# One more large matmul per attention slot and per recurrence chunk, into a PSUM tile that the next product overwrites

## What is computed

```python
# recurrence, over chunks of tokens
scores = einsum('bhtk,bhsk,bhtsk->bhts', q, k, decay)
o = einsum('bhts,bhsv->bhtv', scores, v) + einsum('bhtk,bhkv->bhtv', q * exp(G), S)
S = exp(G_last) * S + einsum('bhsk,bhsv->bhkv', k * exp(G_last - G), v)
# stick-breaking attention of the prompt, causal
z = q @ k.T * scale + bias
sp = where(mask, softplus(z), 0);  after = reverse_cumsum(sp) - sp
o = where(mask, exp(log_sigmoid(z) - after), 0) @ v
```

## Time and profile before

| | us |
|---|---|
| median of three timed runs | 4821.75 (4820.92 to 4822.06) |
| the profiled execution's own time | 4756.05 |
| its span from first to last instruction | 4753.9 |
[...]

### The profile page before, as it was taken

How to read it: one execution, slowest core, us unless ns; L and a number is a source line. 1 busy time by engine, 2 the same in 40 slices (tenths; PEclk the granted TensorE clock), 3 DMA queues, 4 the chain that set the end, 5 groups by cost and what they waited for, 6 DMA issues and landing times.

```text
span 4753.9 us, 42732 instructions
## 1 busy us (share of the span) xinstructions
PE 3042.5 (64%) x12504; PEld 1643.8 (35%) x12504; DVE 2842.7 (60%) x6773; ACT 923.8 (19%) x2045; POOL 2378.1 (50%) x2198
## 2 busy tenths in 40 slices
PE   6877786976675777765646667777465545434434
PEld 3545555644441443332213324443122223101111
DVE  6577831212456556656756766566677657766664
ACT  1432111112231113432101113333110001000000
POOL 1011100000346546657766775567767657777675
PEclk8988996656657777776777786567677767767766
DMA  6476952222669878778999998788999889999998
GB/s 244 168 309 263 395 201 83 52 94 71 236 229 366 307 281 318 286 250 331 333 358 356 371 379 299 276 301 322 348 334 387 333 314 362 348 367 375 351 370 318
DMA packets 432901, 1389.01 MB, mean 292 GB/s; under 512 B 67174, under 2 KB 135014, under 8 KB 420382
## 3 DMA queue, kind: packets, MB, share of 16 engines
q0 software_dynamic: 306432, 1216.48, 68.1%
q1 hardware_dynamic: 102094, 144.95, 9.1%
q10 hardware_dynamic: 24144, 24.86, 1.5%
HBM read 1333.57 MB, written 56.86 MB: 292 GB/s over the span
## 4 chain that ended last, share of the span: by engine, by line
POOL 21%; PE 19%; issue 17%; another core or an unknown queue 6%; DVE 5%; DMA 5%; ACT 2%; ACTq 1%; DVEq 1%; PEld 0%; SPq 0%; PEldq 0%; POOLq 0%
POOL st_rows L1471 21%; PE st_ps_y L1809 3%; PE st_ps_q L1732 3%; PE st_ps_q L1764 3%; DMA st_rows<-in_peer_v,st_expert_v 2%; PE st_ps_m L1709 2%; PE st_ps_t L1718 2%; PE st_ps_m L1741 2%; DMA st_rows<-in_peer_u,st_expert 2%; DVE st_rows L2037 1%; PE st_ps_m L1685 1%; PE st_ps_s L1793 1%; PE st_ps_s L1777 1%; PE st_ps_q L1735 1%
## 5 line engine op out<-in xcount | busy, mean ns | idle before, releaser
L1471 POOL DMA_INDIRECT st_rows<-in_peer_v,st_expert_v x1024 | 1115.7, 1090 | 835.5 <-PE st_ps_y L1809 365.1
L2037 DVE CUSTOM_DVE_ANT_0 st_rows<-st_rows,st_h 128x1024 f32<-128x1024 f32 x1024 | 1232.0, 1223 | 354.2 <-DMA st_rows<-in_peer_u,st_expert 310.8
L1471 POOL DMA_INDIRECT st_rows<-in_peer_u,st_expert x1024 | 1155.4, 1128 | 552.6 <-issue 300.8
L1809 PE MATMUL st_ps_y<-st_rows,st_diag 128*32 128x512 f32 x4096 | 898.0, 728 | 270.1 <-DMA st_rows<-in_peer_v,st_expert_v 112.0
L1809 PEld LDWEIGHTS st_ps_y<-st_rows,st_diag 128*32 128x32 f32 x4096 | 190.2, 127 | 923.1 <-issue 440.3
L1793 PE MATMUL st_ps_s<-st_both,st_pick_tokens 128*128 128x32 f32 (+1 forms) x520 | 114.5, 381 | 594.8 <-DVEq L2083 359.5
L1793 PEld LDWEIGHTS st_ps_s<-st_both,st_pick_tokens 128*128 128x128 f32 x520 | 109.1, 309 | 626.6 <-issue 626.0
L1764 PE MATMUL st_ps_q<-st_shared 128*128 128x128 f32 (+3 forms) x1024 | 277.4, 439 | 72.1 <-issue 69.8
L607 PE MATMUL pd_ps<-pd_w,pd_xnT 128*128 128x256 f32 x1152 | 271.1, 395 | 23.6 <-ACT pd_stage L516 13.2
L1764 PEld LDWEIGHTS st_ps_q<-st_shared 128*128 128x128 f32 x1024 | 204.9, 225 | 149.7 <-issue 99.9
L1709 PE MATMUL st_ps_m<-st_shared,st_incl 128*128 128x256 f32 (+5 forms) x352 | 171.7, 586 | 126.4 <-issue 100.9
(11 more groups left out here) (308 smaller groups left out, 4304.0 us busy)
## 6 DMA issues: line engine op xcount, KB each, us to landing
st_shared<-in_w_pq_heads SPq DMA_DIRECT2D x32, 1024.0 KB
st_rows<-in_peer_u,st_expert POOLq DMA_INDIRECT x1024
st_rows<-in_peer_v,st_expert_v POOLq DMA_INDIRECT x1024
pd_w<-in_w_in SPq DMA_DIRECT2D x14, 1024.0 KB, 12.3
scr_proj<-pd_stage ACTq DMA_DIRECT2D x8, 1152.0 KB
hs_step<-scr_factors SPq DMA_DIRECT2D x40, 208.0 KB
scr_score<-st_sc_out ACTq DMA_DIRECT2D x64, 130.0 KB
st_sc<-scr_score SPq DMA_DIRECT2D x64, 130.0 KB
```

The lines of the kernel that those rows point to most:

```text
L1471: pool.indirect_dma_start(rows[n % R][:, :], None, src, bass.IndirectOffsetOnAxis(ap=idx, axis=0)).then_inc(row_loaded[n % R], 16)
L1809: ins = nc.tensor.matmul(ps_y[j * QUAD:(j + 1) * QUAD, c * 512:(c + 1) * 512], diag[k % 2][:, QS * j + q, :], rows[n % R][:, c * 512:(c + ...
L2037: nc.vector.tensor_tensor_reduce(out=rows[n % R][:, :], in0=rows[n % R][:, :], in1=hb, scale=1.0, scalar=0.0, op0=ALU.mult, op1=ALU.add, a ...
```

## The change

A helper `keep_busy` issues one matmul with `start=True, stop=True`. In `hgrn_steps` it stands in `within(c)`, after the waits and before the four transposes: the stationary operand is the 128 x 128 identity, the moving operand the chunk's 416 factor columns, the output columns 0 to 415 of `ps_k[j]`, which the four transposes overwrite. In `stream` it stands in `attend`, before the logits of tile t+3: identity times the first `BUSY[g]` columns of the key tile, into `ps_q[T % 2]`; `BUSY` is 144, 400, 512, 512 columns for the groups 0 to 3. The logits product overwrites the part of it that ScalarE reads. It is issued once per chunk (40) and once per tile (176). No wait, no transfer and no instruction of another engine is added or moved.

```diff
@@ hgrn_steps, tensor
+            def keep_busy(out, square, data):
+
+                nc.tensor.matmul(out, square, data, start=True, stop=True, skip_group_check=True)
+
             def within(c):
 
                 j = c % 2
@@
                 if c >= 2:
                     pe.wait_ge(kn_ready, c - 1)
                     pe.wait_ge(score_ready, c - 1)
+                keep_busy(ps_k[j][:, 0:4 * H * C], ident[:, :], step[c % 4][:, :, :, :].rearrange("p h k t -> p (h k t)"))
                 for h in range(H):
                     ins = nc.tensor.transpose(ps_k[j][0:C, h * HG_D:(h + 1) * HG_D], step[c % 4][:, h, KE, :], ident[:, :])
@@ stream, tensor
+            BUSY = [min(512, N_META + (attention_blocks(g)[-1] + 1) * P) for g in range(len(MIX_GROUPS))]
+
+            def keep_busy(out, square, data):
+
+                nc.tensor.matmul(out, square, data, start=True, stop=True, skip_group_check=True)
+
             def attend(g, t):
@@
                     if T >= 2:
                         pe.wait_ge(z_ready, T - 1)
+                    keep_busy(ps_q[T % 2][:, 0:BUSY[g]], ident[:, :], kT_t[pc % 2][:, 0:BUSY[g]])
                     ins = nc.tensor.matmul(ps_q[T % 2][0:nk, lo:W], kT_t[pc % 2][d0:d0 + SB_DIM, c0:c0 + nk], qT_t[pc % 2][d0:d0 + SB_DIM, lo:W],
                                            start=True, stop=(kb < b0), skip_group_check=True)
```

## The result

Over 20 runs of each kernel the changed kernel takes 4831.98 us (median) and the kernel before 4803.32: ratio 1.0074, interval 1.0046 to 1.0101. It is slower by 0.7%, against a forecast of 4814 with "faster" as the likeliest side. The profiled execution took 4809.34 us where that of before took 4756.05. Runs of one kernel lie here up to 1% from their median, so I read the 53 us between the two profiles by stages and take only what further runs repeat.

A forecast was written before the change was run, and what follows sets the result against it. TensorE's clock was taken to decide the chunk loop and attention stretches. Terms -41 + 5 + 7 + 13 + 3 + 5 = -8 us on the profiled 4756.05, carried to the timed median 4821.75, gave 4814; range 4700 to 4900.

The forecast's parts named there:

- D: Rival in the chunk loop: the clock stays near 0.6 and the stage gets longer; chance 0.04.
- Chunk loop, -41: Chunk loop: clock rises from 0.59 to 0.90, stage falls from 262 to 221 us; bounds -61 to +53.
- Group 0, +5: Attention of group 0: 16 slots of 144 columns at clock 0.50 add 0 to 7.5 us, taken as +5.
- group 1, +3: Attention dots of group 1: half the slots at each clock level, 157 us against 153.8; bounds -42 to +47.
- Group 3, +7: Attention dots of group 3: 78 slots, a quarter at the lower level, 302 us against 294.4; bounds -52 to +150.
- plus some 1 us a step for the idle starts: Group 3: allowance for steps that begin with TensorE idle, added to 293 us of slots to give 302.
- Group 2, +13: Attention dots of group 2: 62 slots, a fifth at the lower level, 274 us against 261.0; bounds -19 to +142.
- The wait: In attend: with slots at 5.7 us, VectorE's dots wait behind the running sum at L2072, up to 17 us a step.
- Instructions, +5: TensorE's 432 more loads and 432 more matmul instructions: one more idle start of about 6 us, bounds 0 and five.
- A: The forecast case: chunk loop gains some 40 us, slots give most back; -50 to +30, 4770 to 4850 us; chance 0.57.
- B: Rival: the attention slots hold the upper clock level too; about -115 us, 4705; chance 0.20.
- C: Rival: attention slots stay at the lower clock level and the dots wait; +80 us, 4900; chance 0.19.

The follow-up runs named there:

- e1: The kernel before plus the added matmul in the chunk loop alone, none in the attention slots: 4326.45 us, ratio 0.9923.
- e3: e1 with the chunk loop's added matmul over 32 partitions of both operands in place of 128: 4490.3 us beside 4360.32 for the kernel before (one run).
- e2: The kernel before plus the added matmuls in the attention slots alone, none in the chunk loop: 4402.51 us, ratio 1.0099.
- e5: The kernel before, unchanged, run again for its stages on that chip: 4361.86 us.
- e6: The changed kernel run again, with nothing edited: 4368.52 us, ratio 1.001 to the kernel before.
- e12: The kernel before, unchanged, run again on a chip with many idle starts: 4741.4 us.
- e15: The changed kernel run again on a chip with many idle starts: 4817.2 us, ratio 1.011 to the kernel before.
- e4: e2 with the slot's added matmul moved to the slot's end, behind the strict sum, into the other ps_q tile: 4346.78 us, ratio 0.9971.
- e7: e4 plus the chunk loop's added matmul as in the change: 4320.32 us, ratio 0.9908.
- e9: e7 with 208 columns in place of 416 in the chunk loop's matmul and none in group 0: 4764.04 us, ratio 0.998.
- the last two groups: The last two of four groups of follow-up runs, both on one chip; the kernel before took 4793.11 and 4789.43 us there.

## Why the prediction was right and wrong

**What bounds the kernel: right.** TensorE's clock decides the chunk loop (PE busy 196.35 of 205.50 us), and the added rows raise it: 0.97 with 128 rows (e1), 0.50 with 32 (e3). It is not busy time, which was 97% in e3. A clock of the loop that does not answer to the addition, the D of the forecast with its 0.04, is out. No run with 128 rows shows it: the loop is at 0.97, not 0.59, and 53 us shorter, not longer.

**Chunk loop, -41: right, a little small.** -53 in the result, -24 to -40 in the other comparisons: the changed loop takes 205 to 211 us, the unchanged one between 229 and 259, so the size is as much the loop before as the change. The chunk price held (4.98 us for 5.03). The clock was 0.97 for my 0.90. That a clock of 0.59 stands for shares of time at 0.50 and at 1.00, as in my sums for this loop, agrees with the windows of 1 us (208 and 38 of 265).

**Group 0, +5: too small; group 1, +3: right** within 5 us, at -2.0. From its first to its last running sum group 0 takes 45.9 us before and 55.1 after, at 0.50 in both. The other pairs (e1 and e2, e5 and e6, e12 and e15) show 8 to 9 us as well, over the 7.5 that I had as the most it could be.

**Group 3, +7: wrong.** +36 as a stage; the dots took 334.9 us where I had 302. The prices were right (5.87 and 2.99 for 5.7 and 3.1). Of 63 slots 17 ran low (27%, I had a quarter), but 13 more ran mixed. **The step that failed is "plus some 1 us a step for the idle starts".** I sized that term, 9 us, from a single row, the 6.32 us ahead of step 31. But my 302 us were built up from slots and then set against a sum over the dots that holds every idle as well: 54.2 us of it in the kernel before, 63.8 in the changed one. In the terms of my own sum the trace has 69 running sums within the dots, not 78 (the other slots lie outside of them), so (334.9 - 63.8) / 69 = 3.9 us a slot for my 3.76 (the mean of a third low, not a quarter), and 64 us of idle for my 9: 271 + 64, where I had 293 + 9. The idle was missed by 55 us, and the slots outside the dots hid 22 of it. A view of PE's waits on "issue" by stage, which has 39.8 us in group 3, would have shown the term before.

**Group 2, +13: wrong** by the same step. My 62 x 4.4 = 274 us hold no idle at all. The trace has 51 running sums within the dots at (283.8 - 48.9) / 51 = 4.6 us, 235 us in all, and 48.9 us of idle. The two errors nearly cancel in the dots (284 for 274); the other 7 us of the stage's +30 lie outside of them. The low price was too small as well, 7.4 us for my 6.5. In both groups the idle itself hardly grew, by 2 and 10 us. It is the slots that did, by 21 and 31 us. Behind an idle start they run at the lower level and pay 5.9 or 7.4 us instead of 3.9 or 5.2, and in group 2 the added time costs at the upper level too (3.76 us for 2.94). On the chips with hardly any idle starts group 2 still lost 19 and 27 us and group 3 only 8 and 3, so it is the loss of group 3 that goes with the idle starts. That they cause it was not tested by taking them out.

**The wait: wrong.** I had the dots wait behind the running sum at L2072. That wait hardly grew (31 to 36 us in group 3, 23 to 25 in group 2) and is nearly nil in e1, e2 and e6. The one that grew, by 42 and 32 us, is a line earlier, at L2064: VectorE waits for ScalarE, which starts from the logits, and these stand right behind the added product. e4 moves the product behind them and takes 56 us off e2. I had priced where on TensorE the product stands at nothing.

**Instructions, +5: right in kind.** PE's idle within the dots grew by 10 us in group 3 and by 2 in group 2.

**The sum.** -8 forecast, +53 between the profiles, +29 between the medians. Of the 61 us between forecast and profiles, groups 2 and 3 are 17 + 29 = 46, the stages without slots 31 (taken for scatter, above), and the loop, groups 0 and 1 give back 15.

**The rivals.** What came is A: the slots give back the loop's gain and more, and 4832 lies in its 4770 to 4850, at the slow end to which I had given 0.15. B did not come on the chips with hardly any idle starts either (e6: 1.001), so the idle starts that I had named against it are not what it fell with alone. e4 and e7 come nearest to B; they needed the product at another place. C's low slots are in the trace, its size is not, and its wait is another (above): the slots of group 3 cost as much as with a third of them low, about the 30% at which I had it decide. Its marks (over 300 and 330 us in the dots) were met in group 3 and missed in group 2. The chance for "slower", 0.38, was too small for what the trace held: the 101 us of idle within the dots of groups 2 and 3 were there to be read.

**What was to show it.** Loop at 0.9 and 210 to 230 us: 0.97 and 205. Step 31 over 0.7: 0.82. Sums within 20 us of 154, 261 and 294: +3, +23 and +40, one of three.

## What to carry to other kernels

The large extra matmul paid in the chunk loop. There TensorE alone bounds, the clock stood at 0.59 before although TensorE was busy, and two of the five products feed only 26 rows. Cost one by level (here 0.94 us for 416 columns at the upper and 1.73 at the lower), and feed all 128 partitions: with 32 the clock stayed at 0.50 (e3). Look at the clock behind each idle of TensorE: behind the 7.13 us above it was 0.50, and the first slot's product took 2.02 us where a settled one takes 1.08. So add up every idle of a phase in the trace of before, both in the old and in the new sum. Ask which wait of the next engine stands behind the place of the extra product, and try it behind what others wait for: here that alone turned +1.0% into -0.3%, and with the loop's part it gave a gain of 0.9 to 1.3%.

## What the runs showed of the hardware

- The same product with 32 in place of 128 rows fed (1.72 and 1.73 us at 0.50) kept the clock at 0.50 for 363 us at 97% busy; with 128 rows it was 0.97 (e3, e1). Half of the columns gave 0.81 (e9).
- An idle of 7.13 us began at a clock of 1.00; about 5 us into it the clock was 0.50, and it was 1.00 again about 8 us after PE's next instruction. The slots behind it took 5.87, 4.09 and 2.99 us. In the stages of groups 2 and 3 of the first two profiles PE has 66 idles of over 2.5 us; in the first 1 us behind them the clock was 0.50 in 65 and 0.96 in one.
- The same kernel before takes 4360 and 4364 us on two chips and 4789 to 4803 us where the result and the last two groups were measured. The stages without slots take 2128 to 2135 us on the former and 2350 to 2401 on the latter. PE's idle starts in group 3 are 1.3 us in the one profile and 37 to 40 in the others. DMA's share in that stage is 0.92 in the one and 0.82 or 0.83 in the others, which may be the cause or only follow from it. VectorE too waits on "issue" at its two lines of a slot in the latter (32 us in group 3 of the kernel before) and not in e5, so it is not TensorE's alone. What the idle starts wait for, no row names; I tried nothing that would tell, and it stays open.
